# Down projections of a two-block transformer: weight sums by accumulating transfers, six raw places, row differences on VectorE

## The reference

```
f = (silu(h @ w_gate) * (h @ w_up)) @ w_down          # first block
x = x + rms_norm(f, ln_post_ffn)
...
return (silu(gate) * val) @ w_down                    # second block, gate and val after a 3-tap convolution
```

## Time and profile before

| | |
|---|---|
| median of 3 runs | 1316.39 us (1314.7 to 1319.87) |
| the profiled execution, its own time | 1315.77 us |
| its span, first to last instruction | 1313.4 us |
| busy: TensorE, VectorE, ScalarE, GpSimd | 1267.6, 1019.8, 731.9, 620.1 us |
| granted TensorE clock, mean | 0.993 |
| moved from memory | 132.47 MB |
| raw loads of the down projections | 22 of 1 MB, 18 of 512 KB, 18 of 256 KB |

### The profile page before, as it was taken

How to read it: one execution, slowest core, us unless ns; L and a number is a source line. 1 busy time by engine, 2 the same in 40 slices (tenths; PEclk the granted TensorE clock), 3 DMA queues, 4 the chain that set the end, 5 groups by cost and what they waited for, 6 DMA issues and landing times.

```text
span 1313.4 us, 22163 instructions
## 1 busy us (share of the span) xinstructions
PE 1267.6 (97%) x7684; PEld 1145.1 (87%) x7684; DVE 1019.8 (78%) x1728; ACT 731.9 (56%) x1465; POOL 620.1 (47%) x644
## 2 busy tenths in 40 slices
PE   8999999999999988999999999999999999788998
PEld 7999988999999866789999999889889898566787
DVE  6677857899888999985565788368977777999854
ACT  5666745455555545546677788345455455345452
POOL 5655662265655576626767765210232314756100
PEclk9999999999999999999999999999999999999999
DMA  6221213333333353722222333232232323434421
GB/s 203 77 73 57 96 66 96 97 129 98 122 100 96 128 162 121 207 73 73 73 58 65 69 85 107 82 129 64 81 113 80 112 87 114 168 112 149 148 97 64
DMA packets 127944, 135.69 MB, mean 103 GB/s; under 512 B 23885, under 2 KB 110108, under 8 KB 127859
## 3 DMA queue, kind: packets, MB, share of 16 engines
q1 hardware_dynamic: 121536, 126.27, 30.8%
q0 software_dynamic: 6320, 8.31, 2.6%
q10 hardware_dynamic: 2, 0.00, 0.0%
HBM read 132.47 MB, written 2.10 MB: 102 GB/s over the span
## 4 chain that ended last, share of the span: by engine, by line
PE 80%; DVE 17%; ACT 2%; issue 1%; DMA 0%; POOL 0%; DVEq 0%; ACTq 0%
PE ps L2774 13%; PE ps L2775 13%; PE ps L2776 13%; PE ps L2893 6%; PE ps L2900 6%; PE ps L2895 6%; DVE w_lo L2337 6%; DVE st_lo L2348 5%; PE ps L3026 3%; PE ps L3030 3%; PE ps L3028 3%; PE ps L2988 2%; DVE hid L2355 2%; DVE hid L2356 2%; PE ps L2977 2%; PE ps L2976 2%
## 5 line engine op out<-in xcount | busy, mean ns | idle before, releaser
L2774 PE MATMUL ps<-h_hi,w_hi 128*128 128x256 f32 (+1 forms) x748 | 238.4, 319 | 0.0
L2775 PE MATMUL ps<-h_lo,w_hi 128*128 128x256 f32 (+1 forms) x748 | 237.4, 317 | 0.0
L2776 PE MATMUL ps<-h_hi,w_lo 128*128 128x256 f32 (+1 forms) x748 | 237.2, 317 | 0.0
L2893 PE MATMUL ps<-w_hi,h_hi 128*128 128x384 f32 (+2 forms) x512 | 162.6, 328 | 0.0
L2895 PE MATMUL ps<-w_hi,h_lo 128*128 128x384 f32 (+2 forms) x512 | 157.9, 319 | 0.0
L2774 PEld LDWEIGHTS ps<-h_hi,w_hi 128*128 128x128 f32 x748 | 142.6, 191 | 9.6 <-DVE h_lo L2084 0.3
L2776 PEld LDWEIGHTS ps<-h_hi,w_lo 128*128 128x128 f32 x748 | 142.5, 191 | 9.5
L2775 PEld LDWEIGHTS ps<-h_lo,w_hi 128*128 128x128 f32 x748 | 142.6, 191 | 8.5
L3070 PE MATMUL ps<-w_hi,st_hi 128*128 128x512 f32 x252 | 104.9, 416 | 35.0 <-DVE st_lo L2348 28.3
L1218 POOL TENSOR_TENSOR w_lo<-w_raw,w_hi 128x384 fp32r<-128x384 f32 (+2 forms) x114 | 112.9, 1012 | 33.1 <-ACT w_hi L1472 32.9
L1253 POOL TENSOR_TENSOR prob<-prob,rden 128x512 f32<-128x512 f32 (+1 forms) x96 | 71.3, 745 | 65.4 <-DVE rden L2276 65.0
(11 more groups left out here) (327 smaller groups left out, 3547.5 us busy)
## 6 DMA issues: line engine op xcount, KB each, us to landing
w_raw<-in_w_up_dram SPq DMA_DIRECT2D x25, 1024.0 KB, 5.4
w_raw<-in_w_down_dram SPq DMA_DIRECT2D x22, 1024.0 KB, 5.0
w_raw<-in_w_in_dram SPq DMA_DIRECT2D x69, 256.0 KB, 3.5
w_raw<-in_w_gate_dram SPq DMA_DIRECT2D x11, 1024.0 KB, 5.4
w_raw<-in_w_down_dram SPq DMA_DIRECT2D x18, 512.0 KB, 3.7
w_raw<-in_w_out_dram SPq DMA_DIRECT2D x8, 1024.0 KB, 5.0
w_raw<-in_w_up_dram SPq DMA_DIRECT2D x16, 512.0 KB, 3.9
w_raw<-in_w_down_dram SPq DMA_DIRECT2D x18, 256.0 KB, 3.9
```

Source lines behind the costliest of these rows:

```text
L2774: pe.matmul(out_, s_hi, m_hi, start=first and n == 0, stop=False, skip_group_check=True)
L2775: pe.matmul(out_, s_hi, m_lo, start=False, stop=False, skip_group_check=True)
L2776: mm = pe.matmul(out_, s_lo, m_hi, start=False, stop=last and n == len(pairs) - 1, skip_group_check=True)
L2893: pe.matmul(bank, h_hi[:, kb0 + i, tok], hi[:, i, :], start=half == 0 and i == 0, stop=False, skip_group_check=True)
```

## The change

1. **Sums by transfers.** From step 2 on (`SUMMED = 2`) GpSimd makes no weight sum. It issues transfers inside SBUF that add in place: for a four-product step first `raw[1:3] += raw[0], raw[3]`, then `raw[2:4] += raw[1]`, 512 KB written by each, the second waiting for the first; for a three-product step one of 256 KB. T1, T2 and T4 are then a tree instead of a chain and have other signs; the row sums and the saved banks change sign with them. Steps 0 and 1 keep GpSimd's operations, now in place.
2. **Six raw places.** Places 0 and 1 are the old ones (`w_raw`); 2 to 5 (`h_raw`) lie over `h_hi` and `h_lo`, free once product P6 of step 0 is done. `down_place(i)` says which place a step has.
3. **Row differences on VectorE**, in `rows_added`, one step ahead.
4. `down_high` and `down_low` take the raw quarter and T1 in one operation of 128x1024 (`BT`) from step 2 on; T2 and T4 change places and order. The transfers of `early_hi` stand behind steps 5 to 8 instead of 3 to 6, those of `early_lo` behind 13 to 16 instead of 12 to 15.

```diff
+SUMMED = 2
-W_QUARTER = {"P1": 0, "P5": 1, "P6": 2, "P4": 3, "P2": 0, "P3": 1, "P7": 2}
+W_QUARTER = {"P1": 0, "P5": 1, "P6": 3, "P4": 2, "P2": 0, "P3": 1, "P7": 2}
...
+def down_place(i):
+
+    return (1, 0, 2, 3, 4, 5)[(i - 1) % 6] if i else 0
...
+        h_raw = nc.alloc_sbuf_tensor_at("h_raw", [P, 4, 4, 512], F32, offset=h_start)
...
-                        sp.wait_ge(down_sums, weight_sums_at(d, i - 1, 0))
-                        sp.wait_ge(down_lo, weights_lo_at(d, i - 2, 1))
-                    dst, done = down_raw_of(i), down_raw[down_slot(i)]
+                        sp.wait_ge(down_lo, weights_lo_at(d, earlier + 1, 0))
+                        if d and not earlier:
+                            sp.wait_ge(first_sums_lo, 1)
+                    dst, done = down_raw_of(i), down_raw[down_place(i)]
...
+            def down_added_to(d, i, k):
+
+
+                raw, n = down_raw_of(i), down_place(i)
+                if i >= STRASSEN:
+                    dst, src = raw[:, 2, :], raw[:, 1, :]
+                elif k == 0:
+                    dst, src = raw[:, 1:3, :], raw[:, 0:4:3, :]
+                else:
+                    dst, src = raw[:, 2:4, :], raw[:, 1:2, :].to_broadcast([P, 2, 512])
+                if k == 0:
+                    pool.wait_ge(down_raw[n], raw_at(d, i))
+                else:
+                    pool.wait_ge(down_added[n], added_at(d, i, k))
+                pool.dma_start(dst, src, accum_op=ALU.add).then_inc(down_added[n], 16)
+
+            def down_additions(d, i):
+
+                for n, k in ((i - 1, 1), (i, 0)):
+                    if SUMMED <= n < STEPS and (n < STRASSEN or k == 0):
+                        down_added_to(d, n, k)
...
-            for i in range(1, STEPS):
+            for i in range(1, SUMMED):
                 down_sums_of(0, i)
-                if 3 <= i < 3 + EARLY_PARTS:
...
+            for i in range(SUMMED, STEPS):
+                down_additions(0, i)
+                if 5 <= i < 5 + EARLY_PARTS:
...
+                    if i >= 2:
+                        down_high(d, i, "BT")
+                        rows_high(d, i, 0)
+                        rows_high(d, i, 1)
+                        down_high(d, i, "T24")
+                        continue
...
-                link(dve.tensor_tensor(late, late, rows_of_step(i)[:, 1, TOK2], ALU.add))
+                link(dve.tensor_tensor(late, late, rows_of_step(i)[:, 1, TOK2], ALU.subtract))
...
+            def rows_added(d, i):
+
+                rows = rows_of_step(i)
+                if i >= STRASSEN + 2:
+                    dve.wait_ge(rows_lo, rows_at(d, i - 2, 2))
+                dve.tensor_tensor(row_diff[:, i % 2, :, :], halves(rows[:, 1, :]), rows[:, 0:1, TOK1].to_broadcast([P, 2, HALF]),
+                                  ALU.add).then_inc(row_diffs, 1)
...
                 for i in range(start, STRASSEN):
-                    down_low(d, i, "B11")
+                    down_low(d, i, "BT" if i >= 2 else "B11")
...
                 for i in range(STRASSEN, STEPS):
+                    if i == STRASSEN:
+                        dve.wait_ge(row_sums, STRASSEN * d + STRASSEN)
+                        rows_added(d, i)
                     down_low(d, i, "B2")
+                    if i + 1 < STEPS:
+                        rows_added(d, i + 1)
```

More of the change, by code:

```diff
@@ L90, in quarters_free, with before_in_place, added_at, sums @@
     return max(part_at(d, i - 2, name) for name in order_of(d, i - 2) if table[name] in quarters)
-def weight_sums_at(d, i, k):
-    return 4 * STRASSEN * d + 3 * min(i, STRASSEN) + max(i - STRASSEN, 0) + k
+def down_place(i):
+    return (1, 0, 2, 3, 4, 5)[(i - 1) % 6] if i else 0
+def before_in_place(i):
+    earlier = [n for n in range(i) if down_place(n) == down_place(i)]
+    return earlier[-1] if earlier else None
+def weight_sums_at(d, i, k):
+    return 3 * SUMMED * d + 3 * i + k
+def added_at(d, i, k):
+    def sums(n):
+        return 0 if n < SUMMED else 2 if n < STRASSEN else 1
+    same = [n for n in range(STEPS) if down_place(n) == down_place(i)]
+    return 16 * (d * sum(sums(n) for n in same) + sum(sums(n) for n in same if n < i) + k)
 def weights_hi_at(d, i, k):
@@ L114, in raw_at @@
 def raw_at(d, i):
-    return 16 * sum(1 if n < STRASSEN else 2 for e in range(d + 1) for n in range(i % 2, i + 1 if e == d else STEPS, 2))
+    same = [n for n in range(STEPS) if down_place(n) == down_place(i)]
+    return 16 * sum(1 if n < STRASSEN else 2 for e in range(d + 1) for n in same if e < d or n <= i)
 def round_done(j, k=SEVEN):
@@ L808, in two_blocks_kernel @@
         t_sum = sem("t_sum")
-        down_raw = [sem("down_raw0"), sem("down_raw1")]
+        down_raw = [sem(f"down_raw{n}") for n in range(6)]
+        down_added = [sem(f"down_added{n}") for n in range(6)]
         down_sums = sem("down_sums")
@@ L1001, in down_source @@
         def down_source(i, name):
[L1003 to L1008, removed]
+            first, end = W_PIECES[name]
+            return down_raw_of(i)[:, first:end, :].rearrange("p k n -> p (k n)")
         def row_quarters(st, i, first, end):
@@ L1054, in down_loads @@
                 for i in range(STEPS):
-                    src = rows(w)[i % STRASSEN]
+                    src, earlier = rows(w)[i % STRASSEN], before_in_place(i)
                     if i < 2:
@@ L1322, in down_sums_of @@
[L1322 to L1328 removed]
+                raw = down_raw_of(i)
@@ L1437, in _ @@
             down_sums_of(1, 0)
-            first_sums_low("T2", 3)
-            first_sums_low("T4", 4).then_inc(first_sums_lo, 1)
+            first_sums_low("T4", 3)
+            first_sums_low("T2", 4).then_inc(first_sums_lo, 1)
             pool.wait_ge(gate_part, SEVEN * (N_MIXED - 1) + 5)
-            for i in range(1, STEPS):
+            for i in range(1, SUMMED):
                 down_sums_of(1, i)
-                if i == 2:
+            for i in range(SUMMED, STEPS):
+                down_additions(1, i)
+                if i == 6:
                     pool.wait_ge(gate_part, SEVEN * N_MIXED)
@@ L2384, in down_steps @@
                         for a in range(2):
[L2385 removed]
+                            dve.tensor_tensor(kept(1)[:, a], halves(first_two[:, a, :]), halves(bank_of("P4", a)), ALU.add)
             def block_swiglu():
```

93 lines of the change are left out of this document (45 added, 48 removed).

## The result

The changed kernel takes **1348.91 us** (median of four executions, 1347.97 to 1354.02) against 1315.55 for the kernel before on the same chip: a ratio of 1.0256, 95% interval 1.0234 to 1.0278. The profiled execution's span is 1347.5 us against 1313.4, 34.1 more; 17.0 was forecast.

The account below looks back on a forecast made before the run. VectorE, stretched by GpSimd's sums, was taken to bound the down projections. First nine steps +16.2 and +13.3 us, less gains of 6.1 and 6.4 in the last nine, gave +17.0: 1333 us, range 1288 to 1352.

Parts of the forecast that it names:

- What bounds the kernel now: Down projections: VectorE is late, its operations stretched by GpSimd's sums; row sum 1.51 us against 0.42, step period 7.68 us.
- What goes: Without GpSimd's sums, VectorE's four-product step takes 4.7 us, under TensorE's 5.45; in the last nine steps 3.7, under 4.08.
- The price of a transfer: DMA engine time of one 512 KB accumulating transfer: 2.7 us taken, between bounds of 1.47 and 4.6.
- rivals 1 and 2: Accumulate at 1.5 us, nearly a copy's price: 1296 us, chance 0.30; accumulate at 4.6 us, priced by bytes: 1386, chance 0.06.
- rival 1: Accumulate nearly as cheap as a copy, 1.5 us: turn 6.3 us, total 1296, or 1272 if loads hide; chance 0.30.
- The mechanism: First nine steps: TensorE's products wait for VectorE's splits, these for ScalarE, and ScalarE for accumulating transfers; period near 9 us.
- ring turn: GpSimd awaits a step's first transfer, issues its second and the next step's first: one fixed delay, two transfers, part of a load.
- The sum: First nine steps' ends at 530.6 and 1197.0 us, +16.2 and +13.3; with the last nine steps together +17.0 us, 1333.
- The last nine steps: Three-product steps: 9 x 4.08 = 36.7 us plus 2 us of wait for the kept sums; gain 6.1 and 6.4 us.
- The start: Up to the fifth step's first landing: five transfers, five raw loads, one delay, 30.1 us, so 482.3 and 1151.2.
- The turn: First nine steps: 2.1 us delay plus 5.4 for two transfers plus 1.5 for a half-hidden load, 9.0 us.
- the faster case of the first rival: Cheap accumulate with loads hidden as well: TensorE sets the pace, first nine steps end at 501.0 and 1165.3, -44 us, 1272.

Follow-up runs that it names:

- Plain copies: Changed kernel with its transfers copying instead of adding, so its result is wrong: 1320.22 us, ratio 1.0028 to the kernel before.

## Why the prediction came out as it did

**Right.** *What bounds the kernel now* and *What goes*: GpSimd's sums stretch VectorE's operations. Without them the row sums take 0.42 us and the splits 0.68 and 1.23, as forecast; with them put back they take 1.4 to 1.8 again. *The price of a transfer*: A was put at 2.7 us, 2.5 to 2.9 was measured, twice a copy; rivals 1 and 2 fell on this term. Plain copies are rival 1 made real, and gave 1320, not 1296: the price of the transfers was not all of the loss. *The mechanism*, a ring turn in series with TensorE waiting for VectorE, ScalarE and a landing, is what the waits show, and two edits that only keep a transfer queued recovered 22 and 23 us.

**Wrong in size.** 17.1 us are missing, in four terms of *The sum* and *The last nine steps*:

| term | forecast | measured | missed, 1st + 2nd |
|---|---|---|---|
| fifth step's first landing | 482.3; 1151.2 | 486.2; 1172.6 - 15.8 = 1156.8 | 3.9 + 5.6 |
| four turns | 38.5 with the early copies; 36 | 37.7; 38.4 | -0.8 + 2.4 |
| from the last landing to the ninth step's end | 9.8 | 11.4; 10.9 | 1.6 + 1.1 |
| last nine steps | 38.7 | 39.7; 41.1 | 1.0 + 2.4 |

The ninth step's end is here the product at 532.56 (and 1219.08) and twelve matmuls, 2.7 us, as in the forecast. The 15.8 us are the first projection's delay, which shifts the second.

*The start* is the largest miss, and the term that was too small is the raw loads. I counted five of them; six went by. From the first issue to the fifth step's first landing, 452.51 to 486.18 us, are 33.7 us against the forecast's 30.1. The DMA engines' busy tenths between 452 and 485 us, then the queues between 452.5 and 484.6:

```profile
DMA  0019999999998999999999999999999999999991
...
q1 hardware_dynamic: 1632, 6.29, 51.4%
q0 software_dynamic: 1353, 2.61, 46.6%
```

6.29 MB are six loads of 1 MB, 17.6 us at 2.94; the sixth was issued at 473.23 into a place that had just come free. 2.61 MB are five adding transfers, 12.7 us at 2.5. The engines stood idle only before the first packets and between the last ones and the landing, some 3.4 us, where I had 2.1. These add up to the 33.7. The dependence between the transfers cost nothing further in the first projection, because loads filled the time: the transfers behind the first one took 12.2 and 14.7 us to land, but the engines were never idle. The second projection moved the same bytes (6.25 and 2.61 MB between 1138.7 and 1171.4) in 33.9 us, with loads already moving at its beginning and a gap of about 2 us before the landing at 1161.87 instead; its first transfer also went out 1.8 us later than the first projection's delay explains.

*The turn* was 9.0 by the sum and 9.4 to 9.6 measured over those four, but luck had a part in that: its terms were off in both directions. With six loads in the start, no load of 1 MB is left for the turns; what SyncE loads in them is the last nine steps' 768 KB, 2.2 us and not 2.9:

```profile
q1 hardware_dynamic: 1164, 3.20, 27.9%
```

(1172.58 to 1210.95 us, four turns.) I let half of the load hide in the idle time, and none of it does: it is issued at 1172.16, 0.4 us ahead of GpSimd's issue, and both begin to move when the gap ends. By an estimate from the same single prices the idle time was 1.9 us a turn in the second projection, near the 2.1: 38.4 us less 20.3 for eight adding transfers, 9.0 for SyncE's loads and 1.5 for a load of 512 KB on GpSimd's queue, which the forecast had left out, leave 7.6 for four turns.

*The last nine steps* gained 5.1 and 4.0 us, where 6.1 and 6.4 were forecast. The wait for the kept sums stayed at 2.54 and 2.36 us, not 2. In the second projection TensorE's clock adds to it: from 1227.4 us on, behind that wait, matmuls start 0.43 us apart and not 0.23 for three us, 1.6 us lost in all. The four us from 1226, with a granted clock of 0.65, part of them at the lower level of 1.2 GHz:

```profile
1226.00:1230.00 4.00, 4.00 (x13) 3.10 (x13) 3.72 (x7) 1.36 (x2) 1.38 (x2) 0.65 0.73 205
```

The Trainium skill's rule (DMA: Bandwidth & Descriptors, Issuing engines are not separate DMA queues) holds here: between 455 and 475 us the shares of both queues add up to over 1, and a transfer of 512 KB took up to 14.7 us to land where 5.6 was the least. Its fit for transfers that GpSimd issues (the same page, Anatomy of one DMA) would have given the faster case of the first rival: it puts the bytes at 436 GB/s, and an accumulate between two SBUF operands moved 0.62 MB in 3 us, 206 GB/s. The measurement decides; for the accumulate the fit does not stand.

## What to carry to other kernels

Work that is moved to DMA leaves the engines, but where it is a chain, each link pays the landing unless other transfers fill the time; count the links per step, and see that something is queued while one is awaited. When places are added, count anew which loads fall into which stretch: here one more fell into the start, and smaller ones into the turns. Here swapping two issues on one queue was worth 23 us. And a helper that is too slow for all of the work may be right for part of it: of the first nine steps, GpSimd for six and transfers for three (1299 us) beat GpSimd for all nine (1309) and transfers from the third on (1349, or 1326 with the better order).

## What the runs showed of the hardware

- A transfer that adds in place within SBUF costs the DMA engines 2.5 us (2.86 by packet time) per 512 KB, a copy of the same pieces 1.3.
- GpSimd is held 1.2 us to issue an adding transfer (rows of 1.17 to 1.29 us), 0.72 for the copy, 0.86 for an adding one of 256 KB.
- GpSimd's issues alone did not stretch VectorE: a split beside four of them in the changed kernel took 1.23 us. Mixed with its tensor operations they held one for 5.65 us. What holds it that long was not tried apart.
- A dependent pair of transfers with nothing else queued left the DMA engines all but idle between them for 1.6 and 1.2 us in two turns of the changed kernel (1171.4 to 1173.0 and 1181.0 to 1182.2 us), most of it before GpSimd's wait ended.
- TensorE's long waits can cost more than themselves. In the 10 us from 470 on, with 8.04 us idle before the product at 473.35, the granted clock was 0.69, and that matmul took 0.77 us against 0.47 to 0.50 for its like. A mean of 0.69 is part of the stretch at the upper level, 2.4 GHz, and part at the lower, 1.2 GHz.
